# Sample attention of a hybrid decoder step: fewer prompt units in front, four in each sample unit, value transfers issued by GpSimd

## The chip, the core and the metric

The kernel runs on one core of a Trainium2 chip. The metric is the device time of one execution in microseconds (us), lower is better. Before the change it is 1231.96 us, the median of three runs (1231.15 to 1234.93).

## What is computed

One layer of a decoder on 512 prompt tokens and on 64 sample tokens (8 sequences of 8 new tokens with 2048 past positions each). All data is fp32. Cut to the part that matters, each sequence does this:

```
proj = h @ w_in                      # q,k,v of mixer A (8 heads x 64) and of mixer B (4 heads x 128, two q/k maps of 64)
# mixer A: keys at distances (128,1), (512,4), (2048,16), outputs mixed by softmax denominators
# mixer B: (softmax(q1 k1) - lambda softmax(q2 k2)) v over all 2048 past keys (pages of 128 rows) and the new ones
mixed = concat(oa, ob) @ w_o ; x = LN(alpha x + gate1 mixed)
u = h @ w_up ; causal conv ; y = (gelu(a) * g) @ w_down ; x = LN(alpha x + gate2 y)
```

The sample side reads its past keys and values once from HBM: the window caches for mixer A (the rows that a dilated pattern can reach) and 16 pages of 128 rows x 512 values for each sequence of mixer B.

## The kernel before, in words

The program is written engine by engine, with semaphores between them; every engine runs its own list in order. Stages: modulation, input projection (to about 265 us), attention (265 to about 646 us), output projection, up-projection with convolution, down-projection.

The attention stage holds two kinds of work.

- **Prompt units.** `pa` lists 64 of them: a mixer, a head or map, and a block of 128 queries. A unit is scores (PE, L1701), mask and minimum (DVE, L1218 or L1252), exp (ACT, L883 or L894), transposes (PE, L1706), a copy of them (DVE L1226 in front, ACT L903 later), the product with the values (PE, L1712) and its scaling (DVE). The first `NU = 16` run in front, alone, as a pipeline of 19 steps with two buffers of everything. The other 48 (`pb`) go into the sample units, `PER = 3` in each, by `prompt_step` on PE, `probs_b` and `copy_b` on ACT, `mask_b` and `out_b` on DVE; one step of PE weighs unit y-2, turns y-1 and scores y.
- **Sample units.** `sa` lists 16: sequence b, mixer A (m = 0) or B (m = 1), alternating. The keys and values of a unit come in groups of up to four tiles of 128 rows (`groups`): 4, 4, 2 for m = 0 and 4, 4, 4, 4 for m = 1. For a group of keys: SP issues the loads into one of `NK = 3` raw buffers; DVE transposes them in 32 x 32 blocks (`turn_keys`, L1202) into one of three turned buffers; PE scores them (`score_group`, L1768). When all groups and the 8 new keys are scored, DVE takes the least scores (L1297 to L1311), ACT the exponentials (L920 to L926), PE turns the probabilities (L1818, L1821), DVE and ACT copy one half each (L1328, L1330; L944), and PE multiplies them with the values (`weigh_group`, L1799, and L1843 for the new ones) out of one of `NV = 4` value buffers of 1 MB. ACT takes the result (`take_out`, L908).

The value loads (`load_values`, L473, L477, L481) wait until the group four earlier has been weighed. SP issues most of them, in its one queue between the key loads; for m = 1 the groups 2 and 3 are issued by ACT, between the copies and exponentials of the same unit (`values_by_act`). For pages, the issuing engine first reads four page numbers into registers (L459). GpSimd spreads the queries of each unit (L770) and otherwise idles in this stage: it waits for the scores of the unit two earlier.

One iteration w of PE is: prompt step 3w; transposes of unit w; score groups 0 and 1 of unit w+1; prompt step 3w+1; the other groups and the new keys of w+1; weigh groups 0 and 1 of unit w; wait for the least scores of w+1; prompt step 3w+2; weigh the rest of w. DVE turns keys of w+1 in iteration w, between masks and outputs, with the least scores of w at its beginning. The output weights (`w_o`) are loaded after the last sample scores.

The launch line builds the program with `dynamic_dma_scratch_size=1024`, in both kernels. No transfer is issued by GpSimd before.

Of the kernel before, what the change touches and what calls it, by code (L numbers as in the profile page):

```python
# [5 lines left out]
P = 128  # L6
# [3 lines left out]
ALU = mybir.AluOpType  # L10
# [68 lines left out]
def build(nc, a, o, spill):  # L79
# [6 lines left out]
    with ctx:  # L86
# [208 lines left out]
        sa_s = sem("sa_scores")  # L295
# [74 lines left out]
        sa_ph = sem("sa_pt_copied_act")  # L370
        mt_a = sem("mixed_taken_act")
# [11 lines left out]
        NU = 16  # L383
        pb = pa[NU:]
        PER = len(pb) // (2 * DB)
# [45 lines left out]

        def values_by_act(w, g):

            return sa[w][0] == 1 and g >= 2
# [52 lines left out]
        def _(sp):  # L487
# [135 lines left out]
            load_values(sp, 0, 0)  # L623
            load_values(sp, 0, 1)
            load_key_tail(sp, 0)
            load_values(sp, 0, 2)
            for w in range(1, len(sa) + 1):
                here = len(groups[sa[w][0]]) if w < len(sa) else 0
                if here:
                    load_keys(w, 0)  # L630
                    load_keys(w, 1)
                if here == 4:
                    load_keys(w, 2)
                if w >= 2:
                    load_values(sp, w - 1, 0)
                if here == 4:
                    load_keys(w, 3)
                if w >= 2:
                    load_values(sp, w - 1, 1)
                    if sa[w - 1][0] == 0:  # L640
                        load_values(sp, w - 1, 2)
                if here:
                    sp.wait_ge(kn_t, w)
                    load_new_keys(sp, w)
                if w >= 2:
                    sp.wait_ge(sa_pv, w - 1)
                    load_new_values(sp, w - 1)


            sp.wait_ge(sa_s, len(sa))  # L650
# [59 lines left out]
        def _(pool):  # L710
# [55 lines left out]
            for w, (m, b) in enumerate(sa):  # L766
                if w >= 2:
                    pool.wait_ge(sa_s, w - 1)
                for i in range(4):
                    last = nc.gpsimd.tensor_copy(qbd[32 * i:32 * i + 32, w % 2, :, i, :],  # L770
                                                 qrep[32 * i:32 * i + 32, m, :, DS * b:DS * b + DS])
                last.then_inc(q_bd, 1)
            def rest_of_piece(q):

                n, k = PIECES[q]
                if q < 8:
                    pool.wait_ge(wo_high, q + 1)
                else:
                    pool.wait_ge(wl_high, piece_count(q) - 8)
                w = slot(SLOT_OF[n])[:, k:k + 2, :]  # L780
                high, rest = pair_of(n, slice(k, k + 2))
                nc.gpsimd.tensor_tensor(rest, w, high.bitcast(F32), ALU.subtract).then_inc(wl_rest, 1)  # L782
# [28 lines left out]
        def _(act):  # L811
# [98 lines left out]
            act.wait_ge(tail_zero, 1)  # L910
            for w, (m, b) in enumerate(sa):
                n = 32 * sum(groups[m])
                act.wait_ge(sa_min, w + 1)
                for h in range(2):
                    if w >= 1:
                        act.wait_ge(sa_t, 2 * (w - 1) + h + 1)
                    src = sm_s[:, h, 0:n] if m == 0 else bk(h)[:, 0:n]
                    whole = P * (n // P)
                    tiled = p_s[:, h, 0:whole].rearrange("p (u m t) -> p u t m", m=32, t=4)
                    nc.scalar.activation(tiled, src[:, 0:whole].rearrange("p (u t m) -> p u t m", t=4, m=32), ACT.Exp,  # L920
                                         bias=blk_o[:, h:h + 1], scale=-1.0, accum_out=rs_s[:, h, w:w + 1])
                    if n > whole:
                        rest = p_tail[:, h, :].rearrange("p (m t) -> p t m", t=4)[:, 0:2, :]
                        nc.scalar.activation(rest, src[:, whole:n].rearrange("p (t m) -> p t m", m=32), ACT.Exp, bias=blk_o[:, h:h + 1], scale=-1.0,
                                             accum_out=rs_x[:, h, w:w + 1])
                    nc.scalar.activation(p_s[:, h, n:n + 32], sm_n[:, h, :], ACT.Exp, bias=blk_o[:, h:h + 1], scale=-1.0,  # L926
                                         accum_out=rs_n[:, h, w:w + 1]).then_inc(sa_exp, 1)

                if w + 1 < len(sa) and sa[w + 1][0] == 0:
                    load_key_tail(act, w + 1)  # L930
                if w:
                    probs_b(PER * w - 1)
                    copy_b(PER * w - 2)
                    take_out(w - 1)
                if values_by_act(w, 2):
                    load_values(act, w, 2)
                probs_b(PER * w)
                if w:
                    copy_b(PER * w - 1)
# [5 lines left out]
                if values_by_act(w, 3):  # L945
                    load_values(act, w, 3)
                probs_b(PER * w + 1)
                copy_b(PER * w)
            probs_b(len(pb) - 1)
            copy_b(len(pb) - 2)  # L950
            take_out(len(sa) - 1)
            copy_b(len(pb) - 1)
# [78 lines left out]
        def _(dve):  # L1031
# [177 lines left out]
            for s in range(NU + 3):  # L1209
# [27 lines left out]
                if s == 1:  # L1237
                    dve.wait_ge(w_used, CHUNK_AT[("in", 5)] + 1)
                if 1 <= s <= 8:
                    turn_keys(0, (s - 1) // 4, ((s - 1) % 4,))  # L1240
                if s in (12, 14):
                    turn_keys(0, 2, ((s - 12) // 2,))
# [37 lines left out]
            def turn_new(w):  # L1280
                dve.wait_ge(kn_in, 16 * (w + 1))
                if w >= 1:
                    dve.wait_ge(sa_s, w)
# [3 lines left out]
            dve.wait_ge(new_zero, 3)  # L1287
            turn_new(0)
            for w, (m, b) in enumerate(sa):
                n = 32 * sum(groups[m])  # L1290

                dve.wait_ge(sa_s, w + 1)
                if w >= 1:
                    dve.wait_ge(sa_exp, 2 * w)
                for h in range(2):
# [4 lines left out]
                    else:  # L1300
                        then(nc.vector.tensor_reduce(blk[:, h:h + 1], bk(h)[:, 0:n], AX_X, ALU.min))
                here = smask[:, 320 + 32 * m:352 + 32 * m]
                then(nc.vector.tensor_tensor(sm_n, bk(7)[:, 384:448].rearrange("p (h n) -> p h n", h=2),
                                             here[:, None, :].to_broadcast([P, 2, 32]), ALU.add))
                then(nc.vector.tensor_reduce(blk[:, 2:4], sm_n, AX_X, ALU.min))
# [6 lines left out]
                last_g = len(groups[sa[w + 1][0]]) if w + 1 < len(sa) else 0  # L1312
                if last_g:
                    turn_keys(w + 1, 0)
                if w:
                    mask_b(PER * w - 1)
                    out_b(PER * w - 3)
                if last_g:
                    turn_keys(w + 1, 1)
                mask_b(PER * w)  # L1320
                if w:
                    out_b(PER * w - 2)

                full = P * len(groups[m])
# [4 lines left out]
                dve.wait_ge(sa_t, 2 * w + 2)  # L1329
                nc.vector.tensor_copy(ptn[0:32, :, :], bk(4)[0:32, P:3 * P].rearrange("p (h c) -> p h c", h=2)).then_inc(sa_pt, 1)  # L1330
                if last_g:
                    turn_keys(w + 1, 2)
                mask_b(PER * w + 1)
                if w:
                    out_b(PER * w - 1)
                if last_g == 4:
                    turn_keys(w + 1, 3)
                if last_g:
                    turn_new(w + 1)
            mask_b(len(pb) - 1)  # L1340
            out_b(len(pb) - 3)
            out_b(len(pb) - 2)
            out_b(len(pb) - 1)
# [212 lines left out]
        def _(pe):  # L1556
# [228 lines left out]
            def score_new(w):  # L1785
                pe.wait_ge(kn_t, w + 1)
                if w >= 2:
                    pe.wait_ge(pb_o, PER * (w - 1))
                score(w, 0, bk(7), ktn, 384, 32)
                score(w, 1, bk(7), ktn, 416, 32).then_inc(sa_s, 1)  # L1790
# [13 lines left out]
            for g in range(len(groups[0])):  # L1804
                score_group(0, g)
            score_new(0)
            for w, (m, b) in enumerate(sa):
                n = 32 * sum(groups[m])

                prompt_step(PER * w)  # L1810
                for h in range(2):
# [4 lines left out]
                    for u in range(len(groups[m])):  # L1816
                        src = p_tail[:, h, :] if groups[m][u] == 2 else p_s[:, h, P * u:P * u + P]
                        nc.tensor.transpose(bk(2 + h)[:, P * u:P * u + P], src, perm[:, :])  # L1818
                    if h == 0 and w:
                        pe.wait_ge(sa_o, w)  # L1820
                    nc.tensor.transpose(bk(4)[0:32, P + P * h:2 * P + P * h], p_s[:, h, n:n + 32], perm[:, :]).then_inc(sa_t, 1)  # L1821

                nxt = groups[sa[w + 1][0]] if w + 1 < len(sa) else []
                for g in range(len(nxt)):
                    score_group(w + 1, g)
                    if g == 1:
                        prompt_step(PER * w + 1)
                if nxt:
                    score_new(w + 1)
                else:  # L1830
# [3 lines left out]
                for g in range(len(groups[m])):  # L1834
                    weigh_group(w, g)
                    if g == 1:
                        if nxt:
                            pe.wait_ge(sa_min, w + 2)
                        prompt_step(PER * w + 2)
# [6 lines left out]
            prompt_step(len(pb))  # L1846
            prompt_step(len(pb) + 1)
# [265 lines left out]
```

## Time and profile before

| | |
|---|---|
| median of the runs | 1231.96 us |
| the profiled execution, its own time | 1237.05 us |
| its span, first to last instruction | 1235.3 us |
| busy in the span: PE, DVE, POOL, ACT | 1068.6, 830.4, 350.1, 264.2 us |
| mean granted TensorE clock | 0.921 of full speed |
| DMA, mean over the span | 224 GB/s |

```profile
## 2 busy tenths in 40 slices
PE   5699899999688777778765996999999999999994
DVE  1647346625778688777639577467676676998958
ACT  0300000012223323232233103332233232100002
POOL 0433123310000000000007005356664665434323
DMA  8938989863599999998780216375567731413102
```

Each digit is the busy share of one slice of 30.9 us, in tenths; 9 is 90% or more. Slices 9 to 21 are the attention stage. The chain of waits follows the work that ended last back from the end; windows give busy time, granted clock, DMA share and GB/s of a stretch.

### The profile page before, as it was taken

How to read it: one execution, taken by the hardware profiler on the slowest of the kernel's cores; microseconds unless marked ns; L12 is line 12 of the kernel's file. 1: busy time of each engine (PE TensorE's matmuls, PEld its weight loads, DVE VectorE, ACT ScalarE, POOL GpSimd, SP SyncE). 2: the span in 40 equal slices, each digit the busy share in tenths (PEclk: the TensorE clock that was granted, in tenths of full speed). 3: DMA queues.
4: the chain of work that ended last, by engine and by line, in shares of the span. 5: the costliest groups of instructions: out<-in, count | busy, mean ns of one | idle time of the engine just before them, and what ended most of it. 6: DMA issues, size and time to landing. Idle time of an engine off the chain costs nothing.

```text
span 1235.3 us, 23971 instructions
## 1 busy us (share of the span) xinstructions
PE 1068.6 (87%) x9389; PEld 856.7 (69%) x9389; DVE 830.4 (67%) x1497; ACT 264.2 (21%) x588; POOL 350.1 (28%) x378
## 2 busy tenths in 40 slices
PE   5699899999688777778765996999999999999994
PEld 3377577666566555566544875999999999777772
DVE  1647346625778688777639577467676676998958
ACT  0300000012223323232233103332233232100002
POOL 0433123310000000000007005356664665434323
PEclk9799999985899889988886997999999999999997
DMA  8938989863599999998780216375567731413102
GB/s 293 408 135 328 359 329 349 301 238 108 197 366 352 340 344 373 370 327 295 279 305 1 64 38 210 136 266 211 205 232 278 270 105 69 148 57 104 69 19 77
DMA packets 112549, 276.54 MB, mean 224 GB/s; under 512 B 9608, under 2 KB 33174, under 8 KB 108837
## 3 DMA queue, kind: packets, MB, share of 16 engines
q1 hardware_dynamic: 100949, 254.52, 58.2%
q10 hardware_dynamic: 11488, 20.49, 5.0%
q8 instruction: 75, 1.23, 0.4%
q14 instruction: 37, 0.30, 0.1%
HBM read 264.60 MB, written 76.69 MB: 276 GB/s over the span
## 4 chain that ended last, share of the span: by engine, by line
PE 60%; DVE 15%; DMA 11%; ACTq 4%; issue 4%; SPq 2%; ACT 2%; POOL 1%; DVEq 0%; POOLq 0%; PEldq 0%
PE wide L1632 15%; PE wide L1634 15%; PE wide L1633 15%; DMA room<-in_cache_v 3%; PE wide L1768 3%; ACTq L481 3%; PE wide L1712 3%; PE wide L1701 2%; DMA x_sb<-in_cache_v 2%; DMA room<-in_w_ada 2%; DMA ring<-in_w_ada 2%; PE wide L1580 1%; DMA ring<-in_w_down 1%; DVE ring L1202 1%; PE wide L1706 1%
## 5 line engine op out<-in xcount | busy, mean ns | idle before, releaser
L782 POOL TENSOR_TENSOR ring_r<-ring,ring_r 128x1024 fp32r<-128x1024 f32 x70 | 184.6, 2645 | 286.5 <-DVE ring_r L1086 204.3
L1632 PE MATMUL wide<-x_sb_r,ring_r 128*128 128x288 f32 x704 | 211.3, 300 | 8.2 <-DVE ht_r L1108 5.2
L1633 PE MATMUL wide<-ht_r,ring_r 128*128 128x288 f32 x704 | 209.2, 297 | 0.0
L1634 PE MATMUL wide<-x_sb_r,ring_r 128*128 128x288 f32 x704 | 208.4, 296 | 0.0
L1634 PE MATMUL wide<-ring_r,ht_r 128*128 128x512 f32 (+1 forms) x400 | 158.9, 397 | 0.0
L1202 DVE STREAM_TRANSPOSE ring<-ring 128x512 f32<-128x512 f32 x208 | 129.9, 676 | 24.3 <-DMA ring<-in_cache_k 12.2
L1632 PEld LDWEIGHTS wide<-x_sb_r,ring_r 128*128 128x128 f32 x704 | 133.2, 189 | 11.7 <-issue 11.2
L1634 PEld LDWEIGHTS wide<-x_sb_r,ring_r 128*128 128x128 f32 x704 | 134.0, 190 | 0.0
L1633 PEld LDWEIGHTS wide<-ht_r,ring_r 128*128 128x128 f32 x704 | 133.6, 190 | 0.0
L1632 PE MATMUL wide<-ring_r,x_sb_r 128*128 128x512 f32 (+1 forms) x240 | 98.2, 409 | 10.1 <-DVE ht_r L1108 8.7
L770 POOL COPY x_sb<-ring 32x128 f32<-32x128 f32 x64 | 18.4, 287 | 286.4 <-PE wide L1768 284.3
L1633 PE MATMUL wide<-ring_r,x_sb_r 128*128 128x512 f32 (+1 forms) x240 | 95.5, 398 | 0.0
L1632 PE MATMUL wide<-ring_r,ht_r 128*128 128x512 f32 (+1 forms) x220 | 88.2, 401 | 4.3 <-DVE ht_r L1453 2.0
L1634 PEld LDWEIGHTS wide<-ring_r,ht_r 128*128 128x128 f32 (+1 forms) x400 | 72.7, 182 | 21.5
L1633 PE MATMUL wide<-ring_r,ht_r 128*128 128x512 f32 (+1 forms) x220 | 86.7, 394 | 0.0
L1768 PE MATMUL wide<-ring,x_sb 128*32 128x128 f32 (+1 forms) x1792 | 63.4, 296 | 26.2 <-DVE ring L1202 24.7
L1467 DVE SCALAR_TENSOR_TENSOR room<-room,vec_t 128x512 f32<-128x512 f32 x44 | 57.0, 1295 | 41.8 <-ACT room L1003 41.8
L1768 PEld LDWEIGHTS wide<-ring,x_sb 128*32 128x32 f32 x1792 | 51.1, 122 | 39.9 <-DVE ring L1202 30.0
L1712 PE MATMUL wide<-room 128*128 128x128 f32 x320 | 59.7, 325 | 21.8 <-ACT room L903 11.1
L995 ACT ACTIVATE room<-wide,vec_t 128x576 f32<-128x576 f32 x44 | 32.7, 744 | 206.1 <-PE wide L1634 191.9
L1712 PEld LDWEIGHTS wide<-room 128*128 128x128 f32 x320 | 48.6, 223 | 36.1 <-ACT room L903 15.9
L1469 DVE SCALAR_TENSOR_TENSOR room<-room,vec_t 128x512 f32<-128x512 f32 x44 | 69.5, 1579 | 1.6
(231 smaller groups left out, 1892.8 us busy)
## 6 DMA issues: line engine op xcount, KB each, us to landing
ring<-in_cache_k SPq DMA_DIRECT2D x128, 256.0 KB
out_wks<-in_cache_win_k SPq DMA_DIRECT2D x8, 4080.0 KB, 18.9
out_wvs<-in_cache_win_v SPq DMA_DIRECT2D x8, 4080.0 KB, 19.3
ring<-in_w_up SPq DMA_DIRECT2D x22, 1024.0 KB, 7.1
room<-in_w_ada SPq DMA_DIRECT2D x8, 2048.0 KB, 10.5
ring<-in_cache_win_k SPq DMA_DIRECT2D x16, 1024.0 KB
ring<-in_w_in SPq DMA_DIRECT2D x6, 2048.0 KB, 10.7
x_sb<-in_cache_win_v SPq DMA_DIRECT2D x40, 256.0 KB
```

Of the source, the lines that this page charges most:

```text
L481: eng.dma_start(vg[vs][t:P:4, :, :], flat_v[1][bass.ds(pg, 1)].rearrange("a (i m) h d -> m (a i) (h d)", i=4))\
L782: nc.gpsimd.tensor_tensor(rest, w, high.bitcast(F32), ALU.subtract).then_inc(wl_rest, 1)
L995: nc.scalar.activation(u_b[:, k % 2, 2:2 + NT].rearrange("p (h t) -> p h t", h=2), pair, ACT.Identity, bias=vec_t[:, 0, 48 + f:49 + f]).th ...
L1202: last = nc.vector.transpose(ktg[:, G % NK, :, 32 * t:32 * t + 32], kraw[G % NK][:, t, :].rearrange("p (g d) -> p g d", d=32))
L1467: then(nc.vector.scalar_tensor_tensor(out=c_p, in0=u_b[:, k % 2, 1:1 + SEQ], scalar=tap(1), in1=c_p, op0=ALU.mult, op1=ALU.add))
L1469: nc.vector.scalar_tensor_tensor(out=c_p, in0=u_b[:, k % 2, 0:SEQ], scalar=tap(0), in1=c_p, op0=ALU.mult, op1=ALU.add)
L1632: nc.tensor.matmul(out, left[0], right[0], start=first, stop=False)
L1633: nc.tensor.matmul(out, left[0], right[1], start=False, stop=False)
L1634: return nc.tensor.matmul(out, left[1], right[0], start=False, stop=last)
L1701: return nc.tensor.matmul(bank[:, 0:P * (qb + 1)], qt[at, 4 * m + n // 2, P * qb:P * qb + P], kt[at, 4 * m + n // 2, 0:P * (qb + 1)], star ...
L1712: last = nc.tensor.matmul(bank[:, 0:P], pt_b[:, u % 2, P * kb:P * kb + P], vp[:, kb, m, P * (n // 2):P * (n // 2) + P], start=(kb == 0), s ...
L1768: last = nc.tensor.matmul(bank[32 * nn:32 * nn + 32, at:at + nk], qbd[:, w % 2, g].rearrange("p i q -> p (i q)"), keys[:, g, 0:nk], start= ...
```

## The change

The prompt units in front become 4 of 64 and the other 60 go into the sample units, four in each. The order of every engine in the stage is new. PE scores the new keys right after group 0 (they have a semaphore of their own, `sa_ns`, and so have their mask, `sa_nm`, and their transposes, `sa_tn`). DVE turns keys two units ahead, and takes the least scores of unit w+1 inside iteration w (`least(w + 1)`); ACT does the exponentials of w+1 inside iteration w too, one prompt step between the two halves. All value loads go to GpSimd, with the spreading of the next unit's queries behind the first group of each unit. SP keeps the key loads and the new rows. The diff, cut to its core:

```
-        NU = 16
+        NU = 4
-        PER = len(pb) // (2 * DB)
+        PER = 4
 # SP
-            load_values(sp, 0, 0)
-            load_values(sp, 0, 1)
...
-                if w >= 2:
-                    load_values(sp, w - 1, 0)
...
-            sp.wait_ge(sa_s, len(sa))
+            sp.wait_ge(sa_pv, len(sa) - 1)
+            load_new_values(sp, len(sa) - 1)
+            sp.wait_ge(sa_g, NG[len(sa)])
 # GpSimd
+            spread_queries(0)
+            pool.wait_ge(page_in, 16)
+            pool.wait_ge(ada_mm, 12)
+            for w, (m, b) in enumerate(sa):
+                for g in range(len(groups[m])):
+                    load_values(pool, w, g)
+                    if g == 0 and w + 1 < len(sa):
+                        spread_queries(w + 1)
 # ACT
+            probs_s(0, 0)
+            probs_s(0, 1)
+            for w, (m, b) in enumerate(sa):
                 if w:
                     take_out(w - 1)
-                if values_by_act(w, 2):
-                    load_values(act, w, 2)
...
                 nc.scalar.activation(pt_s[:, 1, 0:full], bk(3)[:, 0:full], ACT.Copy).then_inc(sa_ph, 1)
+                step_b(PER * w)
+                step_b(PER * w + 1)
+                if w + 1 < len(sa):
+                    probs_s(w + 1, 0)
+                    step_b(PER * w + 2)
+                    probs_s(w + 1, 1)
+                    if w + 2 < len(sa) and sa[w + 2][0] == 0:
+                        load_key_tail(act, w + 2)
+                    step_b(PER * w + 3)
 # DVE, in front: turn only tiles of group 0, in steps 3 to 6; then
+            turn_new(0)
+            turn_keys(0, 1)
+            turn_keys(0, 2)
+            mask_new(0)
+            turn_keys(1, 0)
+            least(0)
+            turn_keys(1, 1)
+            turn_new(1)
+            turn_keys(1, 2)
+            for w, (m, b) in enumerate(sa):
...
+                step_b(PER * w)
+                if w + 1 < len(sa):
+                    mask_new(w + 1)
+                    if sa[w + 1][0] == 1:
+                        turn_keys(w + 1, 3)
+                    step_b(PER * w + 1)
+                    least(w + 1)
+                    step_b(PER * w + 2)
+                    if w + 2 < len(sa):
+                        turn_keys(w + 2, 0)
+                        turn_keys(w + 2, 1, (0, 1))
+                        turn_new(w + 2)
+                    step_b(PER * w + 3)
+                    if w + 2 < len(sa):
+                        turn_keys(w + 2, 1, (2, 3))
+                        turn_keys(w + 2, 2)
 # PE, iteration w (transposes of w come first)
+                prompt_step(PER * w)
+                if w + 1 < len(sa):
+                    score_group(w + 1, 0)
+                    score_new(w + 1)
+                    score_group(w + 1, 1)
+                    pe.wait_ge(sa_nm, w + 2)
+                    prompt_step(PER * w + 1)
+                    for g in range(2, len(groups[sa[w + 1][0]])):
+                        score_group(w + 1, g)
+                    prompt_step(PER * w + 2)
...
                 for g in range(len(groups[m])):
                     weigh_group(w, g)
+                    if g == 1 and w + 1 < len(sa):
+                        prompt_step(PER * w + 3)
...
-            prompt_step(len(pb))
-            prompt_step(len(pb) + 1)
```

## Rows read from the trace of the kernel before

**Rows 1.** Windows: length, busy (count) of PE, PEld, DVE, ACT, POOL; PEclk, DMA share, GB/s.

```profile
340.00:560.00 220.00, 174.93 (x3349) 129.43 (x3353) 167.66 (x453) 69.99 (x237) 12.63 (x44) 0.90 1.01 353
325.00:645.00 320.00, 247.44 (x4642) 182.88 (x4634) 226.88 (x617) 98.36 (x322) 14.93 (x52) 0.89 0.95 334
265.00:315.00 50.00, 46.50 (x240) 30.66 (x244) 27.07 (x91) 10.68 (x33) 4.29 (x11) 0.62 0.51 172
```

**Rows 2.** DMA issues by transfer: queue, count, KB each.

```profile
ring<-in_cache_k SPq DMA_DIRECT2D x128, 256.0 KB
ring<-in_cache_win_k SPq DMA_DIRECT2D x16, 1024.0 KB
ring<-in_cache_win_k ACTq DMA_DIRECT2D x28, 128.0 KB
```

**Rows 3.** Timeline of PE: start, us; the end of unit 0 and of unit 15.

```profile
338.47 0.41 PE L1843 MATMUL wide<-ht 8*16 8x128 f32 x8
...
639.57 0.62 PE L1843 MATMUL wide<-ht 8*16 8x128 f32 x8
```

**Rows 4.** Chain that ended last, in order of time, in one unit.

```profile
543.27 8.27 DMA x_sb<-in_cache_v
551.58 1.91 PE wide L1799 x32
```

**Rows 5.** Timeline of PE: front's fourth product; unit 0's first scores and transposes.

```profile
280.92 1.92 PE L1712 MATMUL wide<-room 128*128 128x128 f32 x8
...
312.92 2.40 PE L1768 MATMUL wide<-ring,x_sb 128*32 128x128 f32 x96 [0.60 <-issue]
...
319.88 0.69 PE L1818 MATMUL wide<-perm,ht 128*128 128x128 f32 x2 [3.86 <-ACT ht L926]
```

**Rows 6.** Timeline of DVE and ACT around unit 0's least scores; one group turned.

```profile
315.67 0.49 DVE L1297 CUSTOM_DVE_ANT_0 ht<-wide,smask 128x320 f32<-128x320 f32 x1 [2.35 <-PE wide L1768]
318.48 0.76 ACT L920 ACTIVATE ht<-ht,small 128x256 f32<-128x256 f32 x1 [8.81 <-DVE small L1311]
320.88 0.19 ACT L926 ACTIVATION_READ_ACCUMULATOR ht<-ht,small 128x1 f32 x1
522.71 2.49 DVE L1202 STREAM_TRANSPOSE ring<-ring 128x512 f32<-128x512 f32 x4
```

**Rows 7.** Groups by line of PE, 312 to 646 us: busy, mean ns | idle before.

```profile
L1712 PE MATMUL wide<-room 128*128 128x128 f32 x243 | 42.6, 308 | 20.9 <-ACT room L903 11.1 <-DVE small L1311 9.8
L1701 PE MATMUL wide<-room 64*128 64x128 f32 (+3 forms) x96 | 40.3, 501 | 0.0
L1706 PE MATMUL wide<-ident,room 128*128 128x128 f32 x120 | 22.2, 284 | 0.0
```

**Rows 8.** Timeline of DVE and ACT, a unit of mixer B: least scores, exponentials.

```profile
527.68 1.42 DVE L1301 TENSOR_REDUCE small<-wide 128x1 f32<-128x512 f32 x2 [1.90 <-PE wide L1768]
530.78 1.20 ACT L920 ACTIVATE ht<-wide,small 128x512 f32<-128x512 f32 x1 [7.83 <-DVE small L1311]
533.37 0.19 ACT L926 ACTIVATION_READ_ACCUMULATOR ht<-ht,small 128x1 f32 x1
```

**Rows 9.** Instructions of L481 and L770: ns min/median/max; ACT behind one group's issue.

```profile
L481 ACTq DMA_DIRECT2D x_sb<-in_cache_v x32: 609/622/1102, 340.6 to 585.9; - x32
L770 POOL COPY x_sb<-ring x64: 279/286/293, 267.2 to 571.6; 32x128 f32<-32x128 f32 x64
499.42 2.98 ACTq L481 DMA_DIRECT2D room<-in_cache_v  x4
502.50 0.62 ACT L894 ACTIVATE room<-room,mn 128x384 f32<-128x384 f32 x1 [3.67 <-issue]
L782 POOL TENSOR_TENSOR ring_r<-ring,ring_r 128x1024 fp32r<-128x1024 f32 x70 | 184.6, 2645 | 286.5 <-DVE ring_r L1086 204.3
```

**Rows 10.** Timeline behind the last sample unit.

```profile
645.98 0.17 DVE L1345 TENSOR_SCALAR rms<-rms 128x16 f32<-128x16 f32 x1
647.05 2.29 DVE L1353 TENSOR_TENSOR o_all<-o_all,small 128x2048 f32<-128x2048 f32 x1
```

More of the change, by code:

```diff
@@ L370, in build @@
         sa_ph = sem("sa_pt_copied_act")
+        sa_ns, sa_nm, sa_tn = sem("sa_new_scored"), sem("sa_new_masked"), sem("sa_new_transposed")
         mt_a = sem("mixed_taken_act")
@@ L633, in _ @@
                     load_keys(w, 2)
-                if w >= 2:
-                    load_values(sp, w - 1, 0)
+                if w >= 3:
+                    sp.wait_ge(sa_pv, w - 2)
+                    load_new_values(sp, w - 2)
                 if here == 4:
                     load_keys(w, 3)
[L638 to L641, printed above, removed]
                 if here:
@@ L765, in _, with spread_queries @@
             pool.wait_ge(qk_d, len(tr_units) - 2 * TP)
-            for w, (m, b) in enumerate(sa):
+            def spread_queries(w):
+                m, b = sa[w]
                 if w >= 2:
-                    pool.wait_ge(sa_s, w - 1)
+                    pool.wait_ge(sa_g, NG[w - 1])
                 for i in range(4):
@@ L908, in take_out, with step_b, probs_s @@
                 nc.scalar.activation(o_s[:, w, :], bk(4)[:, 0:P], ACT.Copy).then_inc(sa_o, 1)
-            act.wait_ge(tail_zero, 1)
-            for w, (m, b) in enumerate(sa):
+            def step_b(y):
+                if 1 <= y <= len(pb):
+                    copy_b(y - 1)
+                if y < len(pb):
+                    probs_b(y)
+            def probs_s(w, h):
+                m, b = sa[w]
                 n = 32 * sum(groups[m])
                 act.wait_ge(sa_min, w + 1)
[L914 to L930, printed above, removed]
@@ new lines, in probs_s @@
+                if w >= 1:
+                    act.wait_ge(sa_t, 2 * w)
+                    act.wait_ge(sa_tn, w)
+                src = sm_s[:, h, 0:n] if m == 0 else bk(h)[:, 0:n]
+                whole = P * (n // P)
+                tiled = p_s[:, h, 0:whole].rearrange("p (u m t) -> p u t m", m=32, t=4)
+                nc.scalar.activation(tiled, src[:, 0:whole].rearrange("p (u t m) -> p u t m", t=4, m=32), ACT.Exp,
+                                     bias=blk_o[:, h:h + 1], scale=-1.0, accum_out=rs_s[:, h, w:w + 1])
@@ new lines, in probs_s @@
+                if n > whole:
+                    rest = p_tail[:, h, :].rearrange("p (m t) -> p t m", t=4)[:, 0:2, :]
+                    nc.scalar.activation(rest, src[:, whole:n].rearrange("p (t m) -> p t m", m=32), ACT.Exp, bias=blk_o[:, h:h + 1], scale=-1.0,
+                                         accum_out=rs_x[:, h, w:w + 1])
+                nc.scalar.activation(p_s[:, h, n:n + 32], sm_n[:, h, :], ACT.Exp, bias=blk_o[:, h:h + 1], scale=-1.0,
+                                     accum_out=rs_n[:, h, w:w + 1]).then_inc(sa_exp, 1)
@@ L1236, in _ @@
                                             rcp[:, x:x + 1], None, ALU.mult).then_inc(pa_o, 1)
-                if s == 1:
+                if s == 3:
                     dve.wait_ge(w_used, CHUNK_AT[("in", 5)] + 1)
[L1239 to L1242, printed above, removed]
+                if s >= 3:
+                    turn_keys(0, 0, (s - 3,))
             def mask_b(y):
@@ L1282, in turn_new, with mask_new, least @@
                 if w >= 1:
-                    dve.wait_ge(sa_s, w)
+                    dve.wait_ge(sa_ns, w)
                 nc.vector.transpose(ktn[0:32, :, :], kn[0:32, :].rearrange("p (g d) -> p g d", d=32))\
                     .then_inc(kn_t, 1)
[L1287 to L1292, printed above, removed]
+            def mask_new(w):
+                m, b = sa[w]
+                dve.wait_ge(sa_ns, w + 1)
                 if w >= 1:
                     dve.wait_ge(sa_exp, 2 * w)
+                here = smask[:, 320 + 32 * m:352 + 32 * m]
+                then(nc.vector.tensor_tensor(sm_n, bk(7)[:, 384:448].rearrange("p (h n) -> p h n", h=2),
+                                             here[:, None, :].to_broadcast([P, 2, 32]), ALU.add))
+                nc.vector.tensor_reduce(blk[:, 2:4], sm_n, AX_X, ALU.min).then_inc(sa_nm, 1)
+            def least(w):
+                m, b = sa[w]
+                n = 32 * sum(groups[m])
+                dve.wait_ge(sa_g, NG[w + 1])
                 for h in range(2):
@@ L1301, in _ @@
                         then(nc.vector.tensor_reduce(blk[:, h:h + 1], bk(h)[:, 0:n], AX_X, ALU.min))
[L1302 to L1305, printed above, removed]
+                dve.wait_ge(sa_nm, w + 1)
                 then(nc.vector.tensor_tensor(blk[:, 0:2], blk[:, 0:2], blk[:, 2:4], ALU.min))
@@ L1311, in _, with step_b @@
                 nc.vector.transpose(blk_o, blk_r).then_inc(sa_min, 1)
[L1312 to L1322, printed above, removed]
+            def step_b(y):
+                if y < len(pb):
+                    mask_b(y)
+                if 2 <= y < len(pb) + 2:
+                    out_b(y - 2)
+            dve.wait_ge(new_zero, 3)
+            turn_new(0)
[8 more added lines that the diff above has]
+            for w, (m, b) in enumerate(sa):
                 full = P * len(groups[m])
@@ L1787, in score_new @@
                 if w >= 2:
-                    pe.wait_ge(pb_o, PER * (w - 1))
+                    pe.wait_ge(pb_o, PER * (w - 1) - 1)
                 score(w, 0, bk(7), ktn, 384, 32)
-                score(w, 1, bk(7), ktn, 416, 32).then_inc(sa_s, 1)
+                score(w, 1, bk(7), ktn, 416, 32).then_inc(sa_ns, 1)
             def weigh_group(w, g):
@@ L1802, in weigh_group @@
                 last.then_inc(sa_vg, 1)
-            for g in range(len(groups[0])):
-                score_group(0, g)
+            score_group(0, 0)
             score_new(0)
+            score_group(0, 1)
+            score_group(0, 2)
             for w, (m, b) in enumerate(sa):
                 n = 32 * sum(groups[m])
-                prompt_step(PER * w)
                 for h in range(2):
@@ L1817, in _ @@
                         src = p_tail[:, h, :] if groups[m][u] == 2 else p_s[:, h, P * u:P * u + P]
[L1818 to L1828, printed above, removed]
-                    score_new(w + 1)
+                        last = nc.tensor.transpose(bk(2 + h)[:, P * u:P * u + P], src, perm[:, :])
+                    last.then_inc(sa_t, 1)
+                if w:
+                    pe.wait_ge(sa_o, w)
+                for h in range(2):
+                    last = nc.tensor.transpose(bk(4)[0:32, P + P * h:2 * P + P * h], p_s[:, h, n:n + 32], perm[:, :])
+                last.then_inc(sa_tn, 1)
+                prompt_step(PER * w)
+                if w + 1 < len(sa):
+                    score_group(w + 1, 0)
+                    score_new(w + 1)
+                    score_group(w + 1, 1)
[4 more added lines that the diff above has]
+                    prompt_step(PER * w + 2)
                 else:
```

41 lines of the change are left out of this document (4 added, 37 removed).

## Prediction

> **What bounds the kernel now.** I read the table of slices first: between 265 and 646 us, the attention stage, TensorE is at 7 to 9 tenths, DVE at 6 to 7, and DMA at 9 from slice 11 to 18. So no engine fills the stage and the DMA nearly does. The windows say it sharper: from 340 to 560 us the DMA share is 1.01 at 353 GB/s, while PE is busy 174.9 of 220 us and DVE 167.7; from 265 to 315 us, where the 16 prompt units of the front run alone, the DMA share is only 0.51 (172 GB/s) and PE has half its clock for most of it (0.62 in the mean) [rows 1]. Then the bytes: keys are 128 x 256 KB of pages, 16 x 1024 KB of window groups and 32 tails of 128 KB (28 on ACT's queue, the other four on SP's), 54.5 MB, and the values are the same bytes again, 109 MB [rows 2]. For 16 sample units that is 6.8 MB each, 19.3 us at 353 GB/s. The units end 20.07 us apart in the mean: (639.57 - 338.47) / 15 [rows 3]. So the steady part of the stage is within 4% of what the DMA gives.
>
> The chain of waits tells another story on its face: in every unit of mixer B it goes over the value transfers that ACT issues between its other work, and then 8.3 us (elsewhere 8 to 11) of landing, until PE can weigh [rows 4]. A landing of 8 us for 256 KB is a queue in front of it, 1 MB being 3 us at 353 GB/s. An earlier issue lets the transfer queue earlier; it does not make 6.8 MB move faster. I therefore take the late issue by ACT for the form in which a full DMA shows, and not for what the period would fall by.
>
> **The change part by part.**
>
> *Twelve units leave the front.* The product of the fourth unit begins at 280.92 us, that of the sample scores at 312.92 [rows 5]: the front gives up its place from about 280. What then comes first is a chain on DVE, which before had turned unit 0's keys beside the front: turn the new keys (0.7, about one tile's part of a group), groups (0,1) and (0,2), 2.5 and 1.3 us by 2.49 for four tiles, mask 0.5, group (1,0) 2.5, least scores 2.8 (315.67 to 318.48) [rows 6]: 10.3 us. ACT's two exponentials start when the least scores are there, 318.48 to 321.07, 2.6 us, of which half is behind the first transposes [rows 6]. So unit 0's transposes begin at about 280 + 10.3 + 1.3 = 291.6, against 319.88 [rows 5]. Group (1,0) must have landed by 288: ahead of it are the first keys and values, 7.3 MB from 265 us, 21 us at 353 GB/s, so 286 to 288. I add 1.4 us for that: 293.
>
> From there to the end of unit 0 it was 338.9 - 319.9 = 19.0 us [rows 3, 5]. The new iteration has four prompt steps where it had three. A prompt unit costs PE 42.6 + 40.3 + 22.2 us over 48, 2.2 us [rows 7]. And PE, idle for some 10 us behind a short front, may enter it at 1.2 GHz, the level that it had for most of the front (0.62 of 2.4 GHz in the mean of 265 to 315 us) [rows 1]. I take 3 us, from nothing (clock back at once) to 10 (the work of a whole unit at the lower level). 293 + 19 + 2.2 + 3 = 317.2: unit 0 ends 21.7 us earlier.
>
> *Four prompt units in each sample unit.* PE's work per sample unit is 247.4 / 16 = 15.5 us [rows 1] plus 12/16 of 2.2, 1.6: 17.1 us. DVE's is 226.9 / 16 = 14.2 plus about 1. Both stay under 19.3, so the twelve units hide under the DMA. Were that cover gone they would cost 16 x 1.6 = 26 us.
>
> *The new order.* In it the prompt step 4w+3 on PE waits for ACT's copy and exponential of 4w+1 and 4w+2, which stand behind the first exponential of sample unit w+1, which needs its least scores. From the last scores that is 3.1 us (527.68 to 530.78) and 1.3 (half of 530.78 to 533.56) [rows 8], and about 1.5 for copy, exponential and DVE's mask between: 6 to 7.5 us after the last scores. PE covers it with step 4w+2 (2.2) and two groups of weighing (2.1): a stall of 2 to 3 us per unit. 17.1 + 2.5 = 19.6, beside a DMA floor of 19.3. Two limits so close add something: I take a period of 20.0 us, from 19.0 (floor, DMA at the best 60 us) to 21.7 (stall of 4 and a key group late). Against 20.07 that is nothing won: 15 x 0.07 = 1 us.
>
> *Value loads by GpSimd.* 208 transfers (13 per unit), two reads of four page numbers per unit, and 4 copies of 287 ns. SP's and ACT's copies of such a transfer cost 0.62 us each, 0.75 with what lies between four of them (2.98), and ACT was held 3.67 us for one group, so 0.7 for the reads [rows 9]. On GpSimd the price is unknown: no row has a transfer issued there. Below it is bounded by its own smallest instruction here, 0.29 us, above by its largest, 2.65 us [rows 9]. I take 0.8, near the two other queues: 13 x 0.8 + 2 x 0.8 + 1.2 = 13.2 us per unit, less than 20. It decides from (20 - 1.2 - 1.6) / 13 = 1.3 us per transfer. The queries of unit w+1 stand behind the four transfers of (w, 0), which wait for a weighed group; PE needs them some 8 us after that group, and 4 x 0.8 + 1.2 + latency is under 6. ACT is rid of 7.3 us in each pair of units, which it had spare. SP's queue is left with keys and new rows.
>
> One rule of the Trainium skill speaks against this part. Its page "SBUF — State Buffer", in "SBUF: two separate sides", says that GpSimd writes the descriptors of its transfers itself and is locked out while DVE runs a two-port copy from SBUF to SBUF; the page has such a transfer at about 620 ns alone and 3100 beside one. Sixty-four copies of GpSimd in this stage, with DVE busy three quarters of the time, took 279 to 293 ns [rows 9], so what DVE does here (mostly block transposes and reads of PSUM) did not hold that engine. At 620 ns throughout, GpSimd would need 10.9 us per unit, and the sum stays.
>
> *The end.* Before, two prompt steps were left behind the last sample unit: from 639.57 + 0.62 to DVE's scaling at 647.05 it is 6.9 us [rows 3, 10]. Now none is left. ACT's take-out (0.3), the row sums and DVE's three small operations before L1353 need about 2.5: 4.4 us gained. Behind this nothing changes; the output weights are asked for at the last scores as before.
>
> *Sum.* 21.7 + 1 + 4.4 = 27 us: 1237.05 - 27 = 1210 in the profiled execution's own time (1.75 above its span). That execution is 5.1 above the median, so against the median: 1205 us.
>
> **Rivals.**
>
> 1. *The period falls.* Values asked for half a unit earlier let the DMA run without holes. For it: the share was 0.95, not 1, over 325 to 645 us [rows 1], and the chain goes over late issues [rows 4]. Against it: the floor of 19.3. At 19.1: 15 x 0.9 more, 1191 us.
> 2. *The three queues wait for each other.* PE, DVE and ACT each run in order, with the prompt chain now behind the sample's exponentials; a stall of 4 to 5 us gives 21.3 and eats 18 to 20 us: 1224 us. For it: PE already lost 20.9 us before L1712 to ACT and DVE [rows 7].
> 3. *GpSimd becomes the bound* (slower than before). Place: its own queue, in which the query copies stand too. From 1.3 us per transfer the period is its; from 1.42 the 27 us are gone. At 1.6 us the unit takes 23.6 us: 15 x 3.6 = 54 more, 1259; at the bound of 2.65, 37 us, 1460 us. For it: 208 transfers in one queue that also does arithmetic, no row of its price, and a launch line that reserves only 1024 bytes of scratch, so it may have to wait for earlier transfers before it can issue. Against it: the decision point is twice what the other queues pay. By the page's 3100 ns for each one it would be 43 us per unit.
> 4. *Only issue time is saved, and it was covered.* Then the front's 12 units come back as PE time: 20.07 + 1.6 = 21.7, gain 27 - 25: 1230 us. The Trainium skill has the rule behind it, page "DMA: Bandwidth & Descriptors", "Issuing engines are not separate DMA queues": another issuing engine saves only the time to issue. The trace agrees as far as it shows a DMA share of 1.01.
>
> **How the numbers follow.** Forecast (period 19.4 to 20.6) 0.53; rival 1, 0.15; rival 2, 0.09; rival 4, 0.06; rival 3, 0.17. The predicted time is 1205 us. Range 1183 to 1240: below, rival 1 with a faster start; above, rival 2 and 4 whole and the mild part of 3; outside, most of 3 and a little below, 0.2. A measurement of this kernel tells 0.3%, 3.7 us. Faster: the forecast, rivals 1 and 2 and a third of 4, 0.79. Within: half of 4 and the edge of 3, 0.05. Slower: 0.16.
>
> **What would show it.** Right: L1843 of unit 0 near 317 and of unit 15 near 617 us, 20 us apart; DMA share at 1.0 from about 290 on; DVE's L1353 within 3 us of the last L1843; GpSimd's queue idle for 5 us or more in each unit, waiting for weighed groups. Wrong: PE or its weight loads waiting for GpSimd's queries or for values that were asked for late (rival 3); PE waiting for ACT L903 by more than 4 us a unit (rival 2); a period under 19.3 with more than 355 GB/s (rival 1). The prediction as a whole fails if a transfer costs GpSimd over 1.3 us.

## The result and the profile after

The changed kernel takes 1254.91 us (median of 4 runs, 1252.99 to 1257.92), the kernel before 1233.45 us beside it: a ratio of 1.017, 95% interval 1.0129 to 1.0211. It is slower by 21 us, 1.7% (the interval is clear of 1), where 27 us of gain were forecast. The profiled execution took 1253.8 us, 16.8 more than that of before. (Runs of the kernel before ranged from 1220 to 1246 us on the chips used later. So the experiments are read by their ratio to it, and where two of them are compared, the difference by the ratios stands beside that of the times.)

First the windows of the kernel after, of the same two stretches as in [rows 1], and the ends of unit 0 and unit 15 as in [rows 3]. Columns as there.

```profile
340.00:560.00 220.00, 173.55 (x3092) 126.62 (x3092) 155.08 (x443) 73.12 (x240) 77.09 (x159) 0.88 0.84 301
325.00:645.00 320.00, 244.03 (x4281) 177.26 (x4279) 213.58 (x616) 101.58 (x331) 113.56 (x234) 0.86 0.81 288
```

```profile
313.52 0.41 PE L1869 MATMUL wide<-ht 8*16 8x128 f32 x8
...
658.01 0.62 PE L1869 MATMUL wide<-ht 8*16 8x128 f32 x8
```

Unit 0 ends at 313.5 us, 25 earlier than before. But the units are (658.01 - 313.52) / 15 = 22.97 us apart, against 20.07, which takes 43.4 us, and the DMA share fell from 1.01 to 0.84. So the stage left the DMA's floor; something else holds the transfers back. The waits of the kernel after between 265 and 665 us (who waits for whom: us in total, times, longest) name it:

```profile
ACT room L896 <- DVE mn L1257: 121.8, 46, 11.1
DVE ht L1289 <- DMA ht<-ring: 56.7, 8, 8.6
PE wide L1845 <- ACT o_all L910: 37.3, 13, 8.0
PE wide L1821 <- DMA room<-in_cache_v: 14.3, 5, 5.3
PE wide L1869 <- DMA ht<-ring: 6.9, 4, 2.3
```

In these rows loads into `ring` bring key groups, into `x_sb` and `room` values, and into `ht` the new rows; L1845 turns the new part of the probabilities, L1821 and L1869 are the products with past and new values. DVE L1289 is `turn_new`, the transpose of a unit's eight new key rows. It waits 56.7 us in 8 units for a load of 16 KB. Before, the same wait was 2.9 us in all. One of the eight, in the timeline of the kernel after (start, us, instruction, in brackets what ended the idle time before it):

```profile
423.86 1.89 SPq L612 DMA_DIRECT2D ring<-in_cache_k  x4
425.79 0.71 SPq L445 DMA_DIRECT2D ht<-ring  x1
429.91 0.70 DVE L1289 STREAM_TRANSPOSE ht<-ht 32x512 f32<-32x512 f32 x1 [5.55 <-DMA ht<-ring]
430.55 0.64 DVE L1257 CUSTOM_DVE_ANT_0 room<-wide,maskt 128x512 f32<-128x512 f32 x1
431.24 0.72 ACT L896 ACTIVATE room<-room,mn 128x512 f32<-128x512 f32 x1 [8.49 <-DVE mn L1257]
431.96 0.26 ACT L910 ACTIVATE o_all<-wide 128x128 f32<-128x128 f32 x1
432.27 0.61 PE L1845 MATMUL wide<-perm,ht 128*32 128x128 f32 x2 [4.11 <-ACT o_all L910]
432.83 2.74 SPq L609 DMA_DIRECT2D ring<-in_cache_win_k  x2
```

SP asks for the new keys behind the fourth key group of the same unit, whose buffer DVE frees only by turning group 0. So DVE, which has 1.3 us of turning left, comes to `turn_new` before the load is even asked for: 1.4 us of its 5.55 lie before the issue, and 4.1 behind it, in which 1 MB of keys is ahead in the same queue and GpSimd's value transfers run beside it. Units of mixer A have no fourth group, which is why it is 8 units of 16. DVE stands until 429.9 us with a prompt mask, the next key turns and two copies behind it. ACT waits for the mask with its exponential (L896), and `take_out` (L910) stands behind that on ACT. PE waits for `take_out` with the transposes of the new part (L1845). SP itself gets the next free key buffer only at 432.8. So one late load of 16 KB stops DVE, ACT, PE and SP in turn, and with SP the loads of keys. In sum SP waits for key buffers in front of L609 (window keys of mixer A, asked for next) like this:

```profile
SPq L609 <- DVE ring L1209: 62.7, 14, 8.6
```

GpSimd's issue of one value transfer, the price that I had only bounds for, is cheap as an instruction (ns min/median/max; what it waits between them is another matter, see the part on the prediction):

```profile
L477 POOL DMA_DIRECT2D room<-in_cache_v x64: 547/547/563, 281.3 to 650.0; - x64
```

### The profile page after: what moved, and what is told of

Same layout as the page of the kernel before. It is cut to its first block, busy times and chain, and to the rows that moved or that the text cites. A ratio compares the mean times of both kernels' runs of the same rounds, so it can differ in the third digit from the quotient of the medians.

```text
span 1252.1 us, 24023 instructions
## 1 busy us (share of the span) xinstructions
PE 1056.1 (84%) x9389; PEld 848.8 (68%) x9389; DVE 820.3 (66%) x1485; ACT 269.7 (22%) x600; POOL 462.4 (37%) x586
## 4 chain that ended last, share of the span: by engine, by line
PE 59%; DVE 21%; DMA 9%; issue 7%; SPq 3%; POOL 1%; ACT 0%; POOLq 0%; ACTq 0%; DVEq 0%; PEldq 0%
PE wide L1654 16%; PE wide L1656 15%; PE wide L1655 15%; DVE ring L1209 5%; PE wide L1790 4%; DMA ht<-ring 3%; DMA ring<-in_w_ada 2%; PE wide L1734 2%; SPq L612 1%; PE wide L1723 1%; DMA ring<-in_w_down 1%; PE wide L1602 1%; DMA room<-in_w_ada 1%; DVE room L1257 1%; SPq L455 1%
## 5 line engine op out<-in xcount | busy, mean ns | idle before, releaser
L784 POOL TENSOR_TENSOR ring_r<-ring,ring_r 128x1024 fp32r<-128x1024 f32 x70 | 184.0, 2635 | 225.8 <-DVE ring_r L1093 204.7
L477 POOL DMA_DIRECT2D x_sb<-in_cache_v x64 | 35.2, 550 | 99.4 <-issue 98.3
L477 POOL DMA_DIRECT2D room<-in_cache_v x64 | 35.2, 550 | 99.4 <-issue 84.4
L1790 PE MATMUL wide<-ring,x_sb 128*32 128x128 f32 (+1 forms) x1792 | 67.7, 301 | 4.6 <-DVE ring L1209 2.7
L1734 PE MATMUL wide<-room 128*128 128x128 f32 x320 | 56.7, 312 | 16.0 <-ACT room L905 9.7
L731 POOL TENSOR_TENSOR ring_r<-ring,ring_r 128x512 fp32r<-128x512 f32 x24 | 34.1, 1425 | 87.5 <-DVE ring_r L1130 45.0
```

What stands on the lines that cost most here:

```text
L477: eng.dma_start(vg[vs][t:P:4, :, :], flat_v[1][bass.ds(pg, 1)].rearrange("a (i m) h d -> m (a i) (h d)", i=4))\
L1734: last = nc.tensor.matmul(bank[:, 0:P], pt_b[:, u % 2, P * kb:P * kb + P], vp[:, kb, m, P * (n // 2):P * (n // 2) + P], start=(kb == 0), s ...
L1790: last = nc.tensor.matmul(bank[32 * nn:32 * nn + 32, at:at + nk], qbd[:, w % 2, g].rearrange("p i q -> p (i q)"), keys[:, g, 0:nk], start= ...
```

## The experiments

Theory A: the wait for the new keys, which the new order put in DVE's list, sets the pace. Theory B: values come late, because GpSimd holds few transfers in flight. Theory C: the prompt chain between PE, DVE and ACT. Each kernel stands against the kernel before.

**e1: new keys asked for early.** In the kernel after, on SP:

```
                     load_keys(w, 0)
+                    sp.wait_ge(kn_t, w)
+                    load_new_keys(sp, w)
                     load_keys(w, 1)
...
                     load_keys(w, 3)
-                if here:
-                    sp.wait_ge(kn_t, w)
-                    load_new_keys(sp, w)
```

> After, with SP issuing the 16 KB load of unit w's new keys between key groups 0 and 1 of unit w and no longer behind group 3. Theory A (DVE's wait for the new keys, 56.7 us in 8 units of mixer B, sets the pace): that wait falls under 10 us, the distance of units falls from 23.0 to about 20, the time to 1205 to 1220 us. Theory B (values come late since GpSimd holds few transfers in flight): PE's wait for value transfers grows instead, units stay at 22 or more, 1240 us or more. Theory C (PE, DVE and ACT wait for each other through the prompt steps): 1235 to 1250 us.

Measured: 1207.37 us, ratio 0.9819 (0.9787 to 0.985). Two lines moved in one queue give back 47 us (43 by the ratios). The row of DVE's wait for new keys is gone, SP's wait in front of L609 is 15.9 us, and the window and unit ends of this kernel read:

```profile
340.00:560.00 220.00, 184.18 (x3482) 135.39 (x3474) 176.09 (x503) 82.61 (x265) 90.54 (x187) 0.96 0.97 349
```

```profile
313.38 0.62 PE L1868 MATMUL wide<-ht 8*16 8x128 f32 x8
...
609.47 0.63 PE L1868 MATMUL wide<-ht 8*16 8x128 f32 x8
```

The units are 19.74 us apart, 0.4 above the floor of 19.3. Theory A holds. C is out as the cause, for the prompt chain is the same here; B is out too, for PE waits as long for values as in the kernel after (19.1 us in all, 18.6 there). The load still stands behind 1 MB, that of group 0. What changed is that it is asked for before SP waits for the buffer of group 3: new keys that DVE turned at 446.79 us were asked for at 433.44.

**e2: the transpose moved instead.** In the kernel after, `turn_new(w + 2)` goes from behind `turn_keys(w + 2, 1, (0, 1))` to behind `turn_keys(w + 2, 2)`; SP is unchanged.

> After, with DVE's transpose of the new keys of unit w+2 moved from behind half of group 1 to the end of the iteration; SP is unchanged. Theory A: most of the wait goes (the landing is 6 to 8 us, prompt step and 4 us of turning now cover it): 1210 to 1230 us. Theories B and C: within 5 us of 1255.

Measured: 1229.21 us, ratio 0.998 (0.9935 to 1.0026). DVE's wait for new keys is 14.5 us in 7 units. The same cause reached by the other end, and about half of the loss is gone. DVE also waits 19.8 us for key groups (14.6 in e1, 9.1 in the kernel after). What makes up the other half was not taken apart.

**e3: more value transfers in flight.** The kernel after with `dynamic_dma_scratch_size=4096`.

> After, with the scratch reserved for GpSimd's transfers at 4096 instead of 1024 bytes, nothing else. Theory B: GpSimd's idle time between transfers of one group (183 us put down to issue before L477) falls by more than half, PE's wait for values (14.3 and 4.3 us) goes, and the time falls by 10 us or more. Theory A: GpSimd's gaps may go, but the time stays within 4 us of 1255.

Measured: 1287.71 us, ratio 1.047 (1.0435 to 1.0506), a miss for both theories: neither had it slower. PE's wait for values halves: up to 665 us there is none but 0.2 us of its weight loads, and before this stage ends, at 692, come two of 9.1 us in all (18.6 in the kernel after). That B said, but GpSimd's idle time before L477 did not fall (195.9 us, after 182.7), and the 16 KB loads come later still. The waits:

```profile
DVE ht L1289 <- DMA ht<-ring: 91.2, 8, 13.7
PE wide L1845 <- ACT o_all L910: 75.8, 13, 12.8
PE wide L1869 <- DMA ht<-ring: 15.2, 4, 4.6
```

With more value transfers in flight beside it, DVE's wait for a small load grows to as much as 13.7 us. The extra loss has the size of that wait: 34.5 us more of it for 33 us more time. e5 below takes the wait away at this size of scratch.

**e4: one part alone.** The kernel before with the GpSimd part only: `load_values(pool, w, g)` and `spread_queries(w + 1)` as in the change, no value loads on SP and ACT.

> The kernel before, with one part of the change alone: GpSimd issues all value loads and spreads the next unit's queries behind the first group of each; 16 units in front, 3 in each, old orders. Theory A (the value transfers are harmless or help): 1220 to 1234 us. Theory B (values by GpSimd come later): 1245 us or more.

Measured: 1245.17 us, ratio 1.0066 (1.0022 to 1.0109), just at the edge of theory B's 1245 us and a little slower than before. PE waits 29.3 us for values, by the sum of its rows (17.6 before). That speaks for B in the old order: GpSimd's loads help nothing there and cost 0.2 to 1.1%.

**e5: scratch of 4096 with the early new keys.** e1 with `dynamic_dma_scratch_size=4096`.

> e1 (new keys asked for early) with the scratch for GpSimd's transfers at 4096 bytes. Theory A' (more value transfers in flight hurt only because the small loads of new rows queue behind them; the keys' are early now): 1200 to 1212 us, PE's wait for values smaller, its wait for new values larger than in e1. Rival (more value transfers in flight take the DMA from the large key loads too): DVE waits for key groups, 1220 us or more.

Measured: 1228.41 us, ratio 0.9969 (0.9929 to 1.0008). The early load gives back 59 us at this scratch, so most of what e3 lost was the wait for the new keys. But the rival of A' was right too: the time is 21 us (18 by the ratios) over e1. With the keys' small load out of the way, the large ones are late; its waits:

```profile
DVE ring L1208 <- DMA ring<-in_cache_k: 42.2, 21, 8.4
PE wide L1868 <- DMA ht<-ring: 24.7, 7, 5.6
```

In e1 these were 13.3 and 7.6 us (the second row is PE's wait for new values).

**e6: two buffers for the new values.** e1, and (the semaphores and PE's product, which take the two buffers by turns, are left out here):

```
-        vn = part(ht_flat, 3584, 512)
+        vn = [part(ht_flat, 3584, 512), sb("vn2", [P, 512])]
...
-                if w >= 3:
-                    sp.wait_ge(sa_pv, w - 2)
-                    load_new_values(sp, w - 2)
+                if w >= 3:
+                    sp.wait_ge(sa_pv, w - 2)
+                if w >= 2:
+                    load_new_values(sp, w - 1)
```

> e1 with two buffers for the new values, each loaded one unit earlier. In e1 PE waited about 7 us for them in all, and SP's key loads stood behind that wait. Theory A (small loads late are what the order left): 1198 to 1205 us. Rival (the DMA's floor of 19.3 us per unit holds whatever is asked for earlier; e1 is at 19.7): 1205 to 1208 us, no change that can be told.

Measured: 1204.6 us, ratio 0.9754 (0.9706 to 0.9803), and 3 us under e1, which it does not clearly beat: it lies where the two expectations meet and cannot tell them apart. The same kernel once more:

> The same kernel as e6, timed in five rounds, as the version that beats both: 1200 to 1207 us, ratio to the kernel before 0.972 to 0.981.

Measured: 1203.39 us, ratio 0.9789 (0.973 to 0.9849). It beats the kernel before by 2.1%, and by its ratio the kernel after; PE's wait for new values is gone from the waits.

**e7: values back on SP.** e1 with all `load_values` on SP behind `load_keys(w, 3)`, GpSimd only spreads.

> e1 with all value loads back on SP's queue, behind the key loads of the next unit; GpSimd only spreads queries. If GpSimd's queue is what makes the new order work: SP blocks on weighed groups and key groups come late, 1225 us or more. If the order alone does: within 6 us of 1207.

Measured: 1245.07 us, ratio 1.01 (1.0051 to 1.015), 38 us over e1 (35 by the ratios). DVE waits 49.6 us for key groups and PE 41.7 us for new values:

```profile
PE wide L1870 <- DMA ht<-ring: 41.7, 9, 8.5
DVE ring L1210 <- DMA ring<-in_cache_k: 30.9, 13, 5.0
DVE ring L1210 <- DMA ring<-in_cache_win_k: 18.7, 10, 3.9
```

In one queue that waits for weighed groups, keys and new values are asked for too late. So the new order needs a second queue for the values. That it has to be GpSimd's is not shown: the old split between SP and ACT was not tried in the new order.

**e8: 16 units in front again.** e1 with `NU = 16`, four prompt units in each sample unit as long as they last (and the bounds that this needs in `turn_keys` and `prompt_step`).

> e1 with 16 prompt units in front again (48 in sample units, four in each, so that the last four sample units have none). By the prediction's first term: unit 0 ends at about 343 us, 29 us later than in e1; the distance stays at 19.3 to 19.8 us since the DMA sets it: 1228 to 1238 us. Rival (PE's own work sets the distance, 17.1 plus stalls): the last four units run at 17 to 18 us, and the time is 1220 to 1228 us.

Measured: 1241.68 us, ratio 1.0044 (1.0007 to 1.0081), 34 us over e1 (28 by the ratios) and 4 us over the range that was expected. The unit ends of this kernel:

```profile
568.66 0.41 PE L1868 MATMUL wide<-ht 8*16 8x128 f32 x8
...
645.84 0.63 PE L1868 MATMUL wide<-ht 8*16 8x128 f32 x8
```

Unit 0 ends at 347.7 us, 34.3 later than in e1. The last four units, which have no prompt work but the end of its pipeline, are still 77.2 / 4 = 19.3 us apart, and PE is busy 46.9 of the 78 us:

```profile
568.00:646.00 78.00, 46.90 (x1016) 36.50 (x1010) 37.62 (x90) 12.54 (x39) 29.17 (x59) 0.72 0.91 324
```

So PE's work does not set the distance. It is that of the floor, though the DMA share is 0.91 here and not 1. The twelve units in front delay unit 0 by 34 us in the new order, for the 29 expected. The change as a whole brought unit 0 forward by 25 only: in e8 unit 0 ends 9.2 us later than before, with the same 16 units in front. Of these 6.9 lie before its first transposes (326.77 us, before 319.88), for the new order has DVE turn the rest of unit 0's keys behind the front and no longer beside it.

**e9 to e11: the scratch.** e6 with 512, 768 and 1536 bytes. The waits in the table are sums of such rows as above, over 265 to 665 us; with 512 bytes the stage lasts to 708 us, and over the whole of it PE waits 134.5 us for values.

> e6 with the scratch for GpSimd's transfers at 512 bytes. If fewer value transfers in flight only give the key loads more of the DMA: DVE's wait for keys falls, 1198 to 1206 us. If half of the scratch starves the value buffers: PE's wait for values doubles from about 19 us and the time is 1212 us or more.

> e6 with the scratch for GpSimd's transfers at 768 bytes, between 512 (1337 us) and 1024 (1203 us). If the loss grows as transfers in flight get fewer: 1225 to 1290 us, the units 21 to 25 us apart.

> e6 at 1536 bytes, between 1024 (1203 us) and 4096 (1228 us with e1). If key groups lose what value transfers take in flight: 1205 to 1225 us, DVE's wait for key groups over 15 us; if 1024 is still short for the values: under 1200 us.

| bytes | us | ratio to before | DVE waits for key groups | PE waits for values |
|---|---|---|---|---|
| 512 | 1337.33 | 1.089 (1.0822 to 1.0959) | 8.2 us | 112.9 us |
| 768 | 1246.25 | 1.0141 (1.0007 to 1.0275) | 10.5 us | 66.6 us |
| 1024 (e6) | 1204.6 | 0.9754 (0.9706 to 0.9803) | 11.4 us | 19.1 us |
| 1536 | 1225.44 | 0.9984 (0.9943 to 1.0024) | 47.9 us | 7.2 us |

At 512 bytes the second expectation came and at 768 the only one (values starve), at 1536 the first (keys come late, the time at the upper edge of its 1205 to 1225 us). GpSimd's own timeline shows the limit. At 1024 bytes (the e6 kernel, in run e6b, first fence) three transfers go out at once and the fourth 3 us later; at 512 (second fence) it is two and then one at a time:

```profile
444.04 1.64 POOL L469 DMA_DIRECT2D x_sb<-in_cache_win_v  x3
448.66 0.55 POOL L469 DMA_DIRECT2D x_sb<-in_cache_win_v  x1 [2.98 <-issue]
```

```profile
455.01 1.09 POOL L469 DMA_DIRECT2D x_sb<-in_cache_win_v  x2
457.58 0.55 POOL L469 DMA_DIRECT2D x_sb<-in_cache_win_v  x1 [1.48 <-issue]
460.78 0.55 POOL L469 DMA_DIRECT2D x_sb<-in_cache_win_v  x1 [2.66 <-issue]
```

The Trainium skill says on its page "DMA: Bandwidth & Descriptors", in "SWDGE vs HWDGE vs iDMA", that GpSimd writes its descriptors into rings in a reserved part of SBUF. The runs agree that its transfers in flight are limited by this reserve: in front of a later transfer of one group of window values (L469) GpSimd stood 45.5 us in 15 groups in e1, with 1024 bytes, and 0.3 us in e5, with 4096. That a larger one costs 18 to 28 us when other queues carry what is needed first (e5 against e1, e11 against e6), they show by themselves.

## Why the prediction was wrong, by its steps

*The front and unit 0: right, by its steps too.* Group (1,0) was to land at 286 to 288 us and hold DVE, the first transposes to follow at 293:

```profile
286.06 2.49 DVE L1209 STREAM_TRANSPOSE ring<-ring 128x512 f32<-128x512 f32 x4 [5.72 <-DMA ring<-in_cache_k]
292.12 0.69 PE L1840 MATMUL wide<-perm,ht 128*128 128x128 f32 x2 [10.94 <-ACT ht L936]
```

Unit 0 was forecast to end at 317.2 us and did at 313.9 (313.52 + 0.41): of the 24.2 us behind the transposes 21.8 were used.

*Four prompt units under the DMA's floor: right as a limit.* e1 runs at 19.74 us with them, and e8's last four units at 19.3 without.

*The new order: the step that failed.* I worked out the stall of PE behind the exponentials and took a period of 20.0 us, with "from 19.0 ... to 21.7 (stall of 4 and a key group late)". It was 22.97. I followed the large transfers and the prompt chain, and said of SP only that it is "left with keys and new rows". I did not follow the order between SP's `load_new_keys` and DVE's `turn_new`, which now stood before half of key group 1, a mask and the other turns. The term that failed is the wait at nothing for a load of 16 KB; it was 56.7 us in 8 units. Both texts were there; what was missing is the question who is queued behind that wait. Rival 2 had the right kind of mechanism (in-order queues that wait for each other) but the wrong place and 1224 us. With that one wait removed (e1) the time is 1207.4 us for 1205 forecast, but in part by luck. In e1's profile unit 0 ends 25.1 us earlier (for 21.7) and the period of 19.74 gives 5.0 (for 1), while the 4.4 of the end are missing. The stall that I did work out, 2 to 3 us in each unit, is 0.7 there: PE waits 10.3 us in 15 units for ACT's copy (L904).

*Value loads by GpSimd: not what failed, but its price was not the whole of it.* The issue takes 0.55 us for 0.8 and at most 0.69 in the kernel after, also beside a busy DVE; so rival 3 did not come by the price. But with 1024 bytes of scratch GpSimd stands about 3 us in each group of four window values until it can issue the rest (45.5 us in 15 groups in e1), so such a group takes it some 5.2 us, which is 1.3 for each transfer, just where I had put the limit. Its queue was not idle for weighed groups as the sign of being right said: it waits 18.6 us for PE's products in the whole stage and 229.9 with no cause that the profile shows, part of which is this standing. (That limit also has a slip: by my own terms the 27 us are gone from 1.46 us per transfer, not 1.42.) Rival 3's aside on the 1024 bytes was real, but it acts the other way round too: 1024 is near the best of those tried.

*The end: 4.4 us forecast, nothing to speak of got.* Before, 7.5 us lay between the start of the last L1843 and the scaling at 647.05. After, it is 663.97 - 658.01 = 6.0, where I had taken about 2.5 behind the last product. The row sums alone, on PE from 658.57 to 661.31, take 2.7 us, and one small operation of DVE took 1.98, not 0.23 as before. The kernel after there:

```profile
661.54 9.02 POOL L784 TENSOR_TENSOR ring_r<-ring,ring_r 128x1024 fp32r<-128x1024 f32 x3 [11.02 <-ACT ring_r L967]
661.95 1.98 DVE L1373 TENSOR_SCALAR small<-small,lam_s 128x8 f32<-128x8 f32 x1
663.97 4.39 DVE L1375 TENSOR_TENSOR o_all<-o_all,small 128x2048 f32<-128x2048 f32 x1
```

The scaling takes 4.39 us, where it took 2.29 before [rows 10]. GpSimd's subtraction (L784, a part of the output weights) had started first. So it had in e1, e2, e5 and e8, 0.4 us before the small operation, and DVE took 1.98 to 1.99 and 4.39 there too. Before, it started 0.4 us after the scaling, and in e7 after its end, and DVE took 0.23 and 2.29. That one holds the other was only seen in these orders, not tried by itself.

*The sum of the difference*, in the profiled executions: -25.0 (unit 0) + 43.4 (15 distances) - 1.5 + 2.1 (the end) = +19.0, against 16.8 measured; what is behind the stage is thus 2.2 shorter, which was not traced further.

*Ratio of e4.* Why the old order loses a little with GpSimd's loads was not pursued.

## What to carry to other kernels

When the order of several in-order queues is rewritten, list every wait with what now stands behind it, and with what has to be done before the awaited load can be asked for: a load of 16 KB, asked for only once DVE had freed a key buffer and awaited by DVE right behind that, cost some 45 us here, and two moved lines gave it back. In this stage, near the DMA's rate, starting earlier paid (25 us for unit 0), and there is little to be had inside it: e1 is 0.4 us over the floor in each unit. More transfers in flight for one buffer were less for the one that was needed first (e5, e11).

## What the runs showed of the hardware that was not expected

- A GpSimd transfer of 256 KB in 128 rows takes that engine 547 to 563 ns to issue, less than the 0.60 to 0.62 us of SP and ACT before. With a reserve of 1024 bytes it stood about 3 us more in each group of four window values (45.5 us in 15 groups in e1).
- The reserve for GpSimd's transfers changes the time from 1337 us (512 bytes) over 1205 (1024) to 1225 (1536) in one and the same program.
- A DVE operation of 8 columns took 1.98 us beside a GpSimd operation that had started 0.4 us before it, and 0.23 us without one.
